# Triangular solve of a chunked recurrence: X accumulated in PSUM, X^T turned from X by VectorE

## The reference, cut to what matters

```python
def step(state, inp):
    r_t, w_t, k_t, v_t, a_t, b_t = inp
    sa = jnp.einsum("bhvk,bhk->bhv", state, a_t)
    state = (state * w_t[:, :, None, :]
             + sa[..., None] * b_t[:, :, None, :]
             + v_t[..., None] * k_t[:, :, None, :])
    return state, jnp.einsum("bhvk,bhk->bhv", state, r_t)
```

## Time and profile before

| what | value |
|---|---|
| runs of the kernel | median 1353.24 us of 3 (1352.74 to 1355.5) |
| profiled execution | span 1350.5 us from its first to its last instruction; no time of its whole program stands in the record |
| TensorE busy | 1338.2 us, 99% of the span |
| VectorE, ScalarE, GpSimd busy | 846.9, 489.5, 138.2 us |
| granted clock of TensorE | full in all 40 slices |
| DMA | 138.96 MB, mean 103 GB/s |

### The profile page before, as it was taken

How to read it: one execution, slowest core, us unless ns; L and a number is a source line. 1 busy time by engine, 2 the same in 40 slices (tenths; PEclk the granted TensorE clock), 3 DMA queues, 4 the chain that set the end, 5 groups by cost and what they waited for, 6 DMA issues and landing times.

```text
span 1350.5 us, 20607 instructions
## 1 busy us (share of the span) xinstructions
PE 1338.2 (99%) x8808; PEld 1094.4 (81%) x8808; DVE 846.9 (63%) x1139; ACT 489.5 (36%) x767; POOL 138.2 (10%) x153
## 2 busy tenths in 40 slices
PE   9999999999999999999999999999999999999998
PEld 6588988987888888898788888888888787888886
DVE  7377757755467556574665764656666346786654
ACT  6343153042253343444421322313353234344323
POOL 1023114130020110002100000000002111000000
PEclk9999999999999999999999999999999999999999
DMA  5121011023222333122355542222222423122262
GB/s 194 47 78 48 20 48 63 20 95 140 94 94 94 114 124 122 63 94 94 140 188 187 187 157 108 101 93 95 94 94 88 131 101 119 70 81 76 94 172 94
DMA packets 42988, 138.96 MB, mean 103 GB/s; under 512 B 4857, under 2 KB 8569, under 8 KB 42768
## 3 DMA queue, kind: packets, MB, share of 16 engines
q1 hardware_dynamic: 33984, 114.57, 24.7%
q0 software_dynamic: 4864, 17.47, 3.6%
q10 hardware_dynamic: 4048, 5.59, 1.2%
HBM read 131.85 MB, written 2.10 MB: 99 GB/s over the span
## 4 chain that ended last, share of the span: by engine, by line
PE 94%; DVE 2%; DMA 2%; ACT 1%; issue 1%; ACTq 0%; DVEq 0%
PE bank L494 92%; PE bank L497 2%; DMA w_raw<-panels 1%; DVE w_lo L1613 1%; DMA xT<-x 1%; DVE tmp L1613 0%; ACT w_hi L1007 0%; DVE opA_lo L1621 0%; ACT scores L1007 0%; ACT opB_hi L1007 0%; DVE scores L1613 0%; DVE tmp L1621 0%; DVE P L1784 0%; ACT opA_hi L1007 0%; DVE x_tokens L1621 0%
## 5 line engine op out<-in xcount | busy, mean ns | idle before, releaser
L1613 DVE TENSOR_TENSOR w_lo<-w_raw,w_hi 128x1024 fp32r<-128x1024 f32 (+1 forms) x209 | 262.2, 1254 | 330.2 <-ACT w_hi L1007 329.7
L494 PE MATMUL bank<-opA_hi,w_hi 128*128 128x512 f32 x984 | 396.2, 403 | 4.0 <-DVE opA_lo L1621 1.7
L494 PE MATMUL bank<-opA_hi,w_lo 128*128 128x512 f32 x984 | 389.1, 395 | 0.0
L494 PE MATMUL bank<-opA_lo,w_hi 128*128 128x512 f32 x984 | 387.8, 395 | 0.0
L1007 ACT ACTIVATE w_hi<-w_raw 128x1024 fp32r<-128x1024 f32 (+1 forms) x209 | 220.2, 1054 | 351.8 <-DMA w_raw<-panels 351.4
L494 PEld LDWEIGHTS bank<-opA_hi,w_hi 128*128 128x128 f32 x984 | 184.9, 188 | 56.4 <-issue 7.6
L494 PEld LDWEIGHTS bank<-opA_hi,w_lo 128*128 128x128 f32 x984 | 184.9, 188 | 44.7
L494 PEld LDWEIGHTS bank<-opA_lo,w_hi 128*128 128x128 f32 x984 | 185.0, 188 | 43.4 <-issue 1.7
L494 PE MATMUL bank<-opB_hi,w_hi 128*128 128x512 f32 x464 | 184.8, 398 | 0.3 <-DVE w_lo L1613 0.3
L494 PE MATMUL bank<-opB_hi,w_lo 128*128 128x512 f32 x464 | 183.5, 395 | 0.0
L494 PE MATMUL bank<-opB_lo,w_hi 128*128 128x512 f32 x464 | 183.5, 395 | 0.0
(11 more groups left out here) (342 smaller groups left out, 1644.8 us busy)
## 6 DMA issues: line engine op xcount, KB each, us to landing
w_raw<-panels SPq DMA_DIRECT2D x208, 512.0 KB, 3.2
ada_w<-ada POOLq DMA_DIRECT2D x24, 512.0 KB, 4.3
xT<-x ACTq DMA_DIRECT2D x1, 2048.0 KB, 12.3
x_tokens<-x_blocks SPq DMA_DIRECT2D x16, 128.0 KB, 3.7
out<-x_tokens SPq DMA_DIRECT2D x8, 256.0 KB, 2.0
memT<-mem ACTq DMA_DIRECT2D x1, 1024.0 KB, 5.6
w_again<-panels POOLq DMA_DIRECT2D x2, 512.0 KB, 4.9
rotated_q<-P POOLq DMA_DIRECT2D x4, 256.0 KB, 5.3
```

The costliest lines, as they stand in the source:

```text
L494: return pe.matmul(o, lhsT, rhs, start=start, stop=stop, skip_group_check=True)
L1613: return ve.tensor_tensor(o, a, b, op)
```

## The change

Four things are altered in `levels`.

1. X stays summed in its bank. A new `x_started(lane)` multiplies X by the identity into bank 4 + lane (two products of 64 by 64 by 512, one for each half, with start and no stop), and `x_products` of all four rounds add to that bank. ScalarE copies the bank to X after each round and increments `x_level`. `x_added` on VectorE is gone.
2. XT is no longer computed by products in rounds 0 to 3. VectorE turns X into XT in blocks of 32 by 32 (`x_turned`, after `x_level`), and `x_products(n)` for n of 1 and more wait for it by `xt_level`. Up to level 16 X has nothing outside its diagonal blocks of 32, so this is the transpose.
3. The corner of the last level stays a product (`xt_corner`) and a copy (`corner_copied`). The wait for `uv_done`, which frees banks 6 and 7, moves from the first `xt_products` to it.
4. The orders become x 0, x 1, y 0, y 1 on TensorE, and turn 0, mask 0, turn 1, mask 1 on VectorE.

```diff
-X_PRODUCTS = LANES * (2 * (N_LEVELS - 1) + 1)
+X_PRODUCTS = LANES * N_LEVELS
...
+            def x_started(lane):
+                pe.wait_ge(bkt_done, 2 * fs[-1] + 2)
+                for lo, hi in HH:
+                    mm(bank[4 + lane][lo:hi, :], mat("ident")[lo:hi, lo:hi], X[lane][lo:hi, :, :].rearrange("p c l -> p (c l)"),
+                       True, False)
+
             def x_products(n, lane):
                 pe.wait_ge(y_done, lane_count(pair, n, lane, N_LEVELS))
                 if n == 0:
                     pe.wait_ge(xt_done, 3 * fs[lane] + 3)
-                    pe.wait_ge(bkt_done, 2 * fs[-1] + 2)
+                else:
+                    pe.wait_ge(xt_level, XT_STEPS * pair + LANES * (n - 1) + lane + 1)
                 for c in range(NC):
                     for lo, hi in HH:
-                        ins = mm(bank[4 + lane][lo:hi, c * L:(c + 1) * L], XT[lane][lo:hi, c, :], Yt[lane][lo:hi, c, :])
+                        ins = mm(bank[4 + lane][lo:hi, c * L:(c + 1) * L], XT[lane][lo:hi, c, :], Yt[lane][lo:hi, c, :],
+                                 False, n == N_LEVELS - 2)
                 ins.then_inc(x_mm, 1)
...
+            for lane in range(LANES):
+                x_started(lane)
             for n in range(N_LEVELS - 1):
-                x_products(n, 0)
-                xt_products(n, 0)
-                x_products(n, 1)
-                y_products(n + 1, 0)
-                xt_products(n, 1)
-                y_products(n + 1, 1)
+                for lane in range(LANES):
+                    x_products(n, lane)
+                for lane in range(LANES):
+                    y_products(n + 1, lane)
             for lane in range(LANES):
-                xt_products(N_LEVELS - 1, lane)
+                xt_corner(lane)
...
+            for n in range(N_LEVELS - 1):
+                for lane in range(LANES):
+                    ac.wait_ge(x_mm, x_count(pair, n, lane))
+                    act(X[lane][:, :, :], c8(bank[4 + lane][:, :]), ACT.Copy).then_inc(x_level, 1)
...
-            def x_added(n, lane):
-                ve.wait_ge(x_mm, x_count(pair, n, lane, 0))
-                tt(X[lane][:, :, :], X[lane][:, :, :], c8(bank[4 + lane][:, :]), ALU.add).then_inc(x_level, 1)
...
+            def x_turned(n, lane):
+                ve.wait_ge(x_level, lane_count(pair, n, lane, N_LEVELS - 1))
+                ve.transpose(XT[lane][:, :, :].rearrange("p c l -> p (c l)").rearrange("p (b l) -> p b l", l=B),
+                             X[lane][:, :, :].rearrange("p c l -> p (c l)").rearrange("p (b l) -> p b l", l=B)).then_inc(xt_level, 1)
...
             for n in range(N_LEVELS - 1):
-                x_added(n, 0)
-                xt_added(n, 0)
-                x_added(n, 1)
-                y_masked(n + 1, 0)
-                xt_added(n, 1)
-                y_masked(n + 1, 1)
+                for lane in range(LANES):
+                    x_turned(n, lane)
+                    y_masked(n + 1, lane)
                 if n < 3:
                     v_summed(*((0, 1), (1, 0), (1, 1))[n])
```

More of the change, by code:

```diff
@@ L477, in lane_count, with x_count @@
         return LANES * (levels * pair + n) + lane + 1
[L479 to L482, removed]
+    def x_count(pair, n, lane):
+        return X_PRODUCTS * pair + LANES * n + lane + 1
     def columns_before(f):
@@ L708, in x_products, with xt_corner @@
                     pe.wait_ge(xt_done, 3 * fs[lane] + 3)
-                    pe.wait_ge(bkt_done, 2 * fs[-1] + 2)
+                else:
+                    pe.wait_ge(xt_level, XT_STEPS * pair + LANES * (n - 1) + lane + 1)
                 for c in range(NC):
                     for lo, hi in HH:
-                        ins = mm(bank[4 + lane][lo:hi, c * L:(c + 1) * L], XT[lane][lo:hi, c, :], Yt[lane][lo:hi, c, :])
+                        ins = mm(bank[4 + lane][lo:hi, c * L:(c + 1) * L], XT[lane][lo:hi, c, :], Yt[lane][lo:hi, c, :],
+                                 False, n == N_LEVELS - 2)
                 ins.then_inc(x_mm, 1)
[L715 to L719, removed]
+            def xt_corner(lane):
+                n = N_LEVELS - 1
+                pe.wait_ge(uv_done, 5 * fs[-1] + 5)
+                pe.wait_ge(y_done, lane_count(pair, n, lane, N_LEVELS))
                 for c in range(NC):
                     for lo, hi in HH:
[L722 to L726, removed]
+                        ins = mm(bank[6 + lane][lo:lo + B, c * B:(c + 1) * B], Yt[lane][lo + B:hi, c, 0:B],
+                                 XT[lane][lo + B:hi, c, B:L])
                 ins.then_inc(x_mm, 1)
@@ L1930, in y_masked, with corner_copied @@
                     ve.tensor_copy(Yt[lane][:, :, 0:B], c8(bank[2 + lane][:, 0:NC * B])).then_inc(y_done, 1)
-            def x_added(n, lane):
-                ve.wait_ge(x_mm, x_count(pair, n, lane, 0))
-                tt(X[lane][:, :, :], X[lane][:, :, :], c8(bank[4 + lane][:, :]), ALU.add).then_inc(x_level, 1)
[L1936 to L1945, removed]
+            def x_turned(n, lane):
+                ve.wait_ge(x_level, lane_count(pair, n, lane, N_LEVELS - 1))
+                ve.transpose(XT[lane][:, :, :].rearrange("p c l -> p (c l)").rearrange("p (b l) -> p b l", l=B),
+                             X[lane][:, :, :].rearrange("p c l -> p (c l)").rearrange("p (b l) -> p b l", l=B)).then_inc(xt_level, 1)
+            def corner_copied(lane):
+                ve.wait_ge(x_mm, x_count(pair, N_LEVELS - 1, lane))
+                for lo, hi in HH:
+                    ve.tensor_copy(XT[lane][lo:lo + B, :, B:L],
+                                   c8(bank[6 + lane][:, 0:NC * B])[lo:lo + B]).then_inc(xt_level, 1)
             def v_summed(lane, h):
@@ L1964, in levels @@
             for lane in range(LANES):
-                xt_added(N_LEVELS - 1, lane)
+                corner_copied(lane)
             for lane, f in enumerate(fs):
```

## The result

The changed kernel takes 1344.18 us (median of 5 runs, 1342.96 to 1344.97) against 1353.24 us: ratio 0.993, 95% interval 0.9918 to 0.9941. That is 9.06 us less; 8.7 were forecast. Three more rounds of five, on three chips and each beside the kernel before, gave 0.9936, 0.9939 and 0.9932.

What follows compares the result with a forecast made beforehand. TensorE was taken to bound the kernel. Per pair, 7.46 us of removed batches less 2.0 of identity start less about 1.1 of new waiting gives 4.35; two pairs 8.7, so 1353.24 - 8.7 = 1344.5 us, range 1341 to 1349.5.

Steps and rivals of the forecast that it cites:

- The bound: Levels stage: nothing but TensorE limits it, six batches of 0.933 us, 5.60 us a round.
- The identity start: New TensorE work before the first x, not hidden: 2.0 us per pair, between 1.87 and 3.84.
- The round: Levels stage: steady round 4.04 us against 5.60, TensorE idle 0.29 us as lane 1's turn delays its mask.
- The durations: Levels stage: turn 0.69 us, ScalarE copy 0.60, VectorE or ScalarE to TensorE 0.05, batch start to reader 1.15.
- The end of the stage: Last y of lane 0 at 148.19, Z at 151.09 against 155.44; GpSimd's centring covered by 1.6 us.
- The stage: Levels stage 4.35 us shorter per pair: 7.46 less 2.0 less about 1.1 of new waiting.
- What surrounds the span: Median of runs lies 2.74 us above the profiled span, kept unchanged; forecast span 1341.8 us.
- What lies behind the stages: Z, WT, chunk chain and later panel load at 298.70: as before, moving with TensorE, cost taken as nothing.
- B: Identity start: wide products in opposite halves don't overlap, 3.84 us in place of 2.0, 1348.2 us; chance 0.12.
- C: VectorE's turn is slow beside GpSimd, 1.36 us against 0.69, 1.7 us per pair, 1350 us; chance 0.06.
- D: Levels stage with gaps runs at 1.2 GHz, 15 us lost per pair, up to 1383 us; chance 0.07.
- E: After the levels stage, a later stage's end is set by something else, gain given back, about 1353 us; chance 0.06.

Runs made afterwards that it cites:

- psum_only: Kernel before with only X summed in its bank from an identity start and copied by ScalarE, XT still by products: 1356.35 us, ratio 1.0014.
- no_turn: Changed kernel without VectorE's turns of X into XT, so XT stays unfinished and nothing waits for it: 1343.30 us.
- seed_twice: Changed kernel with the identity products that start the sum issued twice in each pair: 1348.31 us.

## Why the prediction was right, step by step

- **The bound.** TensorE alone set the stage: shown by `psum_only`, where VectorE has less to do and the batches keep their 0.933 us.
- **The identity start.** Taken at 2.0 us within 1.87 to 3.84; it is 1.72 us, below my lower end. Eight wide records need 0.215 us each, while the narrow batch that I used as the floor pays for 32 of them. This is the largest error within the stage, 0.28 us per pair.
- **The round.** 4.04 us against 4.06 and 4.07. First round 3.76 against 3.76. The last one, from y(3, 0) at 144.35 to y(4, 0) at 148.51, is 4.16 us, since the batch of 32 by 32 pieces starts 0.1 us behind the pace. The queue of VectorE was the new wait, at the place that was named (lane 1's turn ahead of its mask), 0.3 us: shown by the chain and by `no_turn`.
- **The durations.** Turn 0.69 against 0.71, copy 0.60 against 0.60, from VectorE's end to TensorE 0.05 against 0.06 (138.05 to 138.11), from a batch's start to ScalarE 1.15 against 1.19.
- **The end of the stage.** y(4, 0) to Z 2.90 against 2.86 us; Z does not wait for GpSimd.
- **The stage** 20.90 against 20.75 us in the first pair and 20.85 in the second, **the sum** 8.7 against 8.9 by stages and 9.06 by runs. That it comes so close is in part luck: the start was 0.28 us a pair too dear, the rounds 0.18 too cheap, and the 0.7 to 0.9 us near 590 us were not in it.
- **What surrounds the span.** I kept 2.74 us as what lies around the profiled span. It is 1.3; the rest was a quick execution. This did not enter the gain, but the forecast span of 1341.8 us was missed: it is 1343.6.
- **What lies behind the stages.** I had it unchanged. The chain's panel loads are the same three (290.44, 1039.95 and 1155.68 us now), but TensorE loses 0.67 to 0.94 us near 590 us in every profile of the changed kernel and in neither of the kernel before.
- **The rivals.** B is out by `seed_twice`. C: the turn is not slow beside GpSimd, 0.70 us at 149.59. D: the clock stays at 1.00 within the stage, with its gaps of 0.3 us in each round, but right behind it, from 151.6 us, it fell to 0.50 for 3.4 us in two of the four profiles, at a cost of 1.3 us. The warning that the Trainium skill gives in TensorE: Matmul & The Clock Gate, "A second HAM failure mode: psum-queue depth-cycling", about idle gaps between groups of matmuls is not refuted by that; but such a fall is as frequent in the kernel before, 13 of 65 executions against 4 of 20, so it took nothing from the gain that can be shown. E: a small part is given back, the 0.67 to 0.94 us near 590 us; the rest of the missing 2 us is scatter of single executions.

## What to carry to other kernels

When an engine is busy 100% of a stage, taking whole batches off it pays only down to the next loop of waits: walk one round through all queues before trusting the sum, since eight batches of 0.93 us, 7.5 us of a stage, became 4.4 to 4.5 here. Compare places and not only spans: a delay that stands in every profile of one program is no scatter, and a piece that is longer in one execution alone may be the clock. Look in each engine's order for an instruction that nobody needs yet standing ahead of one that is needed; and before giving work to an idle GpSimd, look whether VectorE works beside it with two inputs from SBUF.

## What the runs showed that I had not expected

- Two VectorE instructions with both inputs in SBUF took 1.78 us each in place of 0.69 while GpSimd added in SBUF; those with one input there kept their time.
- A wide fp32 product of 64 by 64 by 512 in both halves costs less than eight narrow ones: 0.86 us a lane against 0.933.
- The turns alone, with X still added by VectorE, give as much (0.9928) as the whole change (0.993): what the sum in the bank saves VectorE, its start costs TensorE.
- TensorE loses 0.67 to 0.94 us near 590 us, far behind the change, in some of these programs and in others not, with nothing that it waits for; why is open.
- Executions of one kernel differ by 1 to 3 us at a few single places, here a panel load (8.47 against 10.39 us) and a run of TensorE products (6.19 against 7.53 us), the latter since the granted clock was 0.50 for 3.4 us.
